# The first four levels of a triangular inverse: 32x32 block products in four row and column groups, in place of 64x64 products in two halves

## The chip, the cores and the metric

The kernel runs on one core of one Trainium2 chip. The metric is the device time of one execution in microseconds (us). Before the change three runs gave 1793.23 us as the median, from 1792.85 to 1796.31. The profile comes from one more execution, which took 1795.88 us.

## The reference

The reference is a stack of transformer blocks over 256 tokens of width 1024, in float32: two layers of a first kind (feed-forward, a mixer, cross attention, feed-forward), then two of a second kind. The change lies in the mixer of the first kind, in its recurrent branch with 8 heads of 64. Cut to what matters:

```python
def step(state, inp):
    r_t, w_t, k_t, v_t, kk_t, a_t = inp
    sa = jnp.einsum('bhij,bhj->bhi', state, -kk_t)
    state = (state * w_t[:, :, None, :] + sa[..., None] * (kk_t * a_t)[:, :, None, :]
             + v_t[..., None] * k_t[:, :, None, :])
    return state, jnp.einsum('bhij,bhj->bhi', state, r_t)
_, ys = lax.scan(step, state0, xs)          # 256 steps, once in each of the two layers
```

The kernel does not walk 256 steps. It cuts the sequence into 4 chunks of 64 tokens. Within a chunk the steps depend on one another by a strictly triangular 64x64 matrix for each head, and the chunk is solved at once with the inverse of (identity minus that matrix).

## The kernel before

**The whole.** Four engines run programs written out by hand, each strictly in its written order, and semaphores tie them together. TensorE (PE) multiplies; ScalarE (ACT) and VectorE (DVE) split each 128x1024 weight unit into a high part (L337) and a low part (L378), so that three fast products (L398, L399, L400) make one exact one, and they move results out of PSUM. SyncE (SP) streams the units through a ring of 4 buffers.

**The inverse.** Two token tiles `t` (128 partitions each) hold two chunks `c` each, the chunk in partitions 0 to 63 or 64 to 127, and 8 heads beside each other: 32 matrices of 64x64 in all, in `T2[t]`, which holds the inverse so far twice, straight and turned. `dve_rw_inv0` starts it with the inverses of the diagonal 2x2 blocks. Level `lv` (1 to 5) then joins the inverses of diagonal blocks of size 2^lv to such of twice that size. Each of the levels does this, first for t = 0 and then for t = 1 at each step:

- `pe_rw_level`, first loop ("level x"): X = M times T for every head and chunk, into the PSUM bank `x8(t)` (L1261). It waits for the T of the level before.
- `act_rw_level`: ScalarE copies the bank to SBUF, 128x512 (L1280).
- `pe_rw_level`, second loop ("level"): T times X into the same bank (L1273). It waits for that copy.
- `dve_rw_level`: VectorE takes only the new off-diagonal blocks over into T by a mask (COPY_PREDICATED, L1288), and for levels 1 to 4 transposes T by 32x32 blocks (STREAM_TRANSPOSE, L1292).

The masks `low1` to `low4` lie wholly within 32x32 diagonal blocks; `up5`, for level 5, is the 32x32 block off the diagonal.

**Products in halves.** Each product is 64x64 with 64 moving columns, from partitions of one chunk into the same partitions of PSUM. So two of them, c = 0 and c = 1, stand in different row and column groups of the array. A float32 product is two matmul instructions and two weight loads in the trace.

**What stands between the levels.** On PE, after level 2 and after level 3, 8 transposes of a "by token" matrix each (L1181); after level 4 the bonus products (L1417) and half a gate (L1429, L1430); then level 5, and the chunks of the recurrence (L1307 to L1370) with weight units between them. On VectorE each of the levels 1 to 4 is followed or preceded by a 128x1024 product (L1168, L1171, L1158) or a split (L378), in the order `dve_mix` has them:

```python
self.dve_rw_level(l, 1)
self.dve_rw_end(l, 0)
self.dve_split(1)
self.dve_rw_level(l, 2)
self.dve_rw_end(l, 1)
self.dve_rw_level(l, 3)
self.dve_rw_bonus(l)
self.dve_split(1)
self.dve_rw_level(l, 4)
self.dve_rw_level(l, 5)
```

On ScalarE a weight split (L337) stands before the copies of level 2 and of level 4.

Of the kernel before, what the change touches and what calls it, by code (L numbers as in the profile page):

```python
# [13 lines left out]
P = 128  # L14
# [8 lines left out]
HD = 64  # L23
# [108 lines left out]
class Program:  # L132
# [1118 lines left out]

    def pe_rw_level(self, l, lv):
        pe, m = self.nc.tensor, self.rw_pe
        for t in range(NT):
            pe.wait_ge(*self.rw_dve("T", l, t, lv - 1))
            if lv == 1:
                pe.wait_ge(*self.rw_dve("masked", l, 1, 2 * t))
            for h in range(8):
                for c in range(2):
                    co = slice(c * HD, (c + 1) * HD)  # L1260
                    ins = pe.matmul(self.x8(t)[co, h, :], self.MK[co, t, 2 * (h % 4) + h // 4, 0, :], self.T2[t][co, 1, h, :],  # L1261
                                    start=True, stop=True, skip_group_check=True)
            m.mark(ins, "level x", l, t, lv)
        for t in range(NT):
            T, X = self.T2[t], self.XG[t]
            pe.wait_ge(*self.rw_act("X", l, t, lv))
            if lv > 1:
                pe.wait_ge(*self.rw_dve("turned", l, t, lv - 1))
            for h in range(8):
                for c in range(2):  # L1270
                    co = slice(c * HD, (c + 1) * HD)
                    pair = (T[co, 0, h, :], X[co, h, :]) if lv < 5 else (X[co, h, :], T[co, 0, h, :])
                    ins = pe.matmul(self.x8(t)[co, h, :], *pair, start=True, stop=True, skip_group_check=True)  # L1273
            m.mark(ins, "level", l, t, lv)

    def act_rw_level(self, l, lv):
# [2316 lines left out]
```

## Time and profile before

| | |
|---|---|
| median of three runs | 1793.23 us |
| profiled execution | 1795.88 us, of it span 1794.6 |
| PE busy | 1771.5 us (99% of the span) |
| VectorE busy | 1153.2 us (64%) |
| ScalarE busy | 945.4 us (53%) |
| levels 1 to 4 of the inverse, layer 0 | 311.0 to 329.4 us |
| level 5, layer 0 | 333.3 to 338.8 us |
| levels 1 to 4, layer 1 | 934.4 to 952.8 us |
| level 5, layer 1 | 956.7 to 960.6 us |

### The profile page before, as it was taken

To read this page: it belongs to the slowest core of one execution; us is meant where nothing else is said; L and a number is where in the kernel's file an instruction comes from. 1 tells how busy PE (TensorE), PEld (TensorE's weight loads), DVE (VectorE), ACT (ScalarE), POOL (GpSimd) and SP (SyncE) were. 2 spreads that over 40 slices of the span, in tenths; PEclk is the share of its full clock that TensorE was granted. 3 is DMA by queue.
4 is the path that set the end of the run, shared out by engine and by line. 5 is a ranking of instruction groups with operands and counts; after the bars stand their busy time and mean duration, and the time that the engine had idled before them with its cause. 6 is when DMAs were issued, how large, how long until landed. Compare 5 with 4: busy or idle time off the path is not lost.

```text
span 1794.6 us, 26440 instructions
## 1 busy us (share of the span) xinstructions
PE 1771.5 (99%) x10810; PEld 1481.1 (83%) x10810; DVE 1153.2 (64%) x1577; ACT 945.4 (53%) x1433; POOL 130.1 (7%) x90
## 2 busy tenths in 40 slices
PE   9999999999999999999999999999999999999999
PEld 6888888878888888888888878888888888888887
DVE  5555688576555565556786755555697557697556
ACT  6454675345544454447653455444656554656553
POOL 0000010141000001000002310000002000002000
PEclk9999999999999999999999999999999999999999
DMA  8755542123555557545421336555554555554553
GB/s 288 279 187 188 176 143 93 61 94 119 189 186 187 188 185 250 187 170 188 141 84 61 127 110 228 188 188 171 169 176 157 172 188 192 179 176 152 174 187 133
DMA packets 84344, 301.14 MB, mean 168 GB/s; under 512 B 9728, under 2 KB 10880, under 8 KB 83712
## 3 DMA queue, kind: packets, MB, share of 16 engines
q1 hardware_dynamic: 80192, 289.44, 47.2%
q10 hardware_dynamic: 3712, 8.56, 1.4%
q8 instruction: 86, 1.41, 0.3%
q0 software_dynamic: 320, 1.45, 0.2%
q14 instruction: 34, 0.28, 0.0%
HBM read 298.36 MB, written 1.05 MB: 167 GB/s over the span
## 4 chain that ended last, share of the span: by engine, by line
PE 89%; DVE 6%; ACT 3%; issue 1%; DMA 1%; SPq 0%; DVEq 0%; ACTq 0%
PE ps L398 25%; PE ps L400 25%; PE ps L399 25%; DVE wlo L378 2%; PE ps L621 1%; PE ps L1273 1%; PE ps L1261 1%; DMA raw<-stream 1%; DVE a_lo L474 1%; ACT whi L337 1%; PE ps L2668 1%; PE ps L807 1%; PE ps L458 1%; PE ps L421 1%; PE ps L419 1%
## 5 line engine op out<-in xcount | busy, mean ns | idle before, releaser
L378 DVE TENSOR_TENSOR wlo<-raw,whi 128x1024 fp32r<-128x1024 f32 (+1 forms) x545 | 669.6, 1237 | 359.7 <-ACT whi L337 358.1
L337 ACT ACTIVATE whi<-raw 128x1024 fp32r<-128x1024 f32 (+1 forms) x545 | 570.9, 1053 | 455.7 <-PE ps L400 427.1
L398 PE MATMUL ps<-whi,a_hi 128*128 128x512 f32 x1712 | 678.5, 396 | 6.4 <-DVE a_lo L2003 2.0
L400 PE MATMUL ps<-whi,a_lo 128*128 128x512 f32 x1712 | 665.9, 389 | 0.0
L399 PE MATMUL ps<-wlo,a_hi 128*128 128x512 f32 x1712 | 665.0, 388 | 0.0
L398 PEld LDWEIGHTS ps<-whi,a_hi 128*128 128x128 f32 x1712 | 322.2, 188 | 75.8 <-issue 5.2
L400 PEld LDWEIGHTS ps<-whi,a_lo 128*128 128x128 f32 x1712 | 321.8, 188 | 67.5
L399 PEld LDWEIGHTS ps<-wlo,a_hi 128*128 128x128 f32 x1712 | 322.5, 188 | 61.4
L398 PE MATMUL ps<-whi,h_hi 128*128 128x512 f32 x336 | 131.7, 392 | 0.0
L400 PE MATMUL ps<-whi,h_lo 128*128 128x512 f32 x336 | 131.0, 390 | 0.0
L399 PE MATMUL ps<-wlo,h_hi 128*128 128x512 f32 x336 | 130.9, 389 | 0.0
L398 PEld LDWEIGHTS ps<-whi,h_hi 128*128 128x128 f32 x336 | 63.1, 188 | 13.6 <-issue 0.7
L419 PE MATMUL ps<-a_hi,whi 128*128 128x256 f32 x256 | 74.0, 289 | 0.0
L400 PEld LDWEIGHTS ps<-whi,h_lo 128*128 128x128 f32 x336 | 63.1, 188 | 13.2
L399 PEld LDWEIGHTS ps<-wlo,h_hi 128*128 128x128 f32 x336 | 63.1, 188 | 12.9
L420 PE MATMUL ps<-a_lo,whi 128*128 128x256 f32 x256 | 72.4, 283 | 0.0
L421 PE MATMUL ps<-a_hi,wlo 128*128 128x256 f32 x256 | 72.4, 283 | 0.0
L643 ACT ACTIVATE arena<-ps,small 128x256 f32<-128x256 f32 x88 | 36.9, 470 | 65.6 <-PE ps L400 65.5
L551 POOL TENSOR_TENSOR small<-small,minus_half 128x2 f32<-128x2 f32 x9 | 6.3, 700 | 858.0 <-DVE small L544 641.2
L689 DVE SCALAR_TENSOR_TENSOR arena<-ps,small,arena 128x256 f32<-128x256 f32 x88 | 38.5, 479 | 38.3 <-ACT arena L643 38.3
L650 ACT ACTIVATE h_hi<-ps 128x256 fp32r<-128x256 f32 x72 | 23.7, 382 | 57.3 <-PE ps L621 57.3
L788 POOL TENSOR_TENSOR small<-small,minus_half 128x16 f32<-128x16 f32 (+1 forms) x14 | 39.2, 2803 | 165.7 <-DVE small L2610 80.5
(332 smaller groups left out, 1688.4 us busy)
## 6 DMA issues: line engine op xcount, KB each, us to landing
raw<-stream SPq DMA_DIRECT2D x545, 512.0 KB, 3.3
arena<-rows ACTq DMA_DIRECT2D x2, 1026.0 KB, 14.8
arena<-mem_turned ACTq DMA_DIRECT2D x2, 1024.0 KB, 9.0
arena<-lora ACTq DMA_DIRECT2D x2, 768.0 KB, 6.5
arena<-x_turned SPq DMA_DIRECT2D x4, 256.0 KB, 5.9
x_res<-x SPq DMA_DIRECT2D x2, 512.0 KB, 9.1
arena<-mem ACTq DMA_DIRECT2D x1, 1024.0 KB, 14.2
arena<-rows ACTq DMA_DIRECT2D x2, 512.0 KB, 4.8
```

Of the source, the lines that this page charges most:

```text
L337: self.split_hi.mark(act.activation(self.weights(self.whi, u), self.weights(self.raw, u), ACT.Copy), u)
L378: self.split_lo.mark(dve.tensor_tensor(self.weights(self.wlo, u), self.weights(self.raw, u), self.weights(self.whi, u).bitcast(F32), ALU.s ...
L398: pe.matmul(out, a_h, hi, start=start, stop=False, skip_group_check=True)
L399: pe.matmul(out, a_h, lo, start=False, stop=False, skip_group_check=True)
L400: last = pe.matmul(out, a_l, hi, start=False, stop=True, skip_group_check=True)
L419: pe.matmul(out, hi, self.AHI[:, kt, :], start=first and kt == 0, stop=False, skip_group_check=True)
L420: pe.matmul(out, hi, self.ALO[:, kt, :], start=False, stop=False, skip_group_check=True)
L421: last = pe.matmul(out, lo, self.AHI[:, kt, :], start=False, stop=True, skip_group_check=True)
L643: self.silu.mark(act.activation(self.SG[:, t, :], self.bank((2 if j == 1 else 4) + t, 256), ACT.Silu, scale=self.rs(0, t)), key, j, t)
L650: self.ht_hi.mark(act.activation(self.h_place(j)[0][:, kk, :], self.bank(self.h_bank(j, kk), S), ACT.Copy), key, j, kk)
L689: self.h_ready.mark(dve.scalar_tensor_tensor(self.h_buffer(j)[:, t, :], self.bank((2 if j == 1 else 4) + t)[:, 256:512], self.rs(0, t), se ...
L788: m.mark(pool.tensor_tensor(x, x, self.minus_half[:, 0:x.shape[1]], ALU.pow), key)
```

## The change

For the levels 1 to 4 `size` becomes 32, and the list `blocks` has four pairs: rows 0 to 31 with columns 0 to 31, rows 32 to 63 with columns 32 to 63, rows 64 to 95 with columns 0 to 31, rows 96 to 127 with columns 32 to 63. Those are the four diagonal 32x32 blocks of the two chunks. The blocks off the diagonal are no longer computed; the bank keeps there what it held, ScalarE copies it along, and nothing reads it before level 5 has written the whole. In level 5 `size` is 64, and the list has the same two products as before. ScalarE, VectorE, GpSimd and SP are not touched; waits and signals stay where they were.

```diff
+        size = HD // 2 if lv < 5 else HD
+        blocks = [(slice(r, r + size), slice(r % HD, r % HD + size)) for r in range(0, P, size)]
         for t in range(NT):
...
             for h in range(8):
-                for c in range(2):
-                    co = slice(c * HD, (c + 1) * HD)
-                    ins = pe.matmul(self.x8(t)[co, h, :], self.MK[co, t, 2 * (h % 4) + h // 4, 0, :], self.T2[t][co, 1, h, :],
-                                    start=True, stop=True, skip_group_check=True)
+                for rows, cols in blocks:
+                    ins = pe.matmul(self.x8(t)[rows, h, cols], self.MK[rows, t, 2 * (h % 4) + h // 4, 0, cols],
+                                    self.T2[t][rows, 1, h, cols], start=True, stop=True, skip_group_check=True)
...
             for h in range(8):
-                for c in range(2):
-                    co = slice(c * HD, (c + 1) * HD)
-                    pair = (T[co, 0, h, :], X[co, h, :]) if lv < 5 else (X[co, h, :], T[co, 0, h, :])
-                    ins = pe.matmul(self.x8(t)[co, h, :], *pair, start=True, stop=True, skip_group_check=True)
+                for rows, cols in blocks:
+                    pair = (T[rows, 0, h, cols], X[rows, h, cols]) if lv < 5 else (X[rows, h, cols], T[rows, 0, h, cols])
+                    ins = pe.matmul(self.x8(t)[rows, h, cols], *pair, start=True, stop=True, skip_group_check=True)
```

The next rows are PE's order in the first layer, from the last weight unit ahead of the inverse to level 2 and the first transposes; - is before, + is after, and a count is one of products in the source, of which the trace has two instructions each:

```order
 L400 MATMUL ps<-whi,a_lo 128x512
-L1261 MATMUL ps<-arena 64x64 x32
-L1273 MATMUL ps<-arena 64x64 x32
-L1261 MATMUL ps<-arena 64x64 x32
-L1273 MATMUL ps<-arena 64x64 x32
+L1262 MATMUL ps<-arena 32x32 x64
+L1273 MATMUL ps<-arena 32x32 x64
+L1262 MATMUL ps<-arena 32x32 x64
+L1273 MATMUL ps<-arena 32x32 x64
 L1181 MATMUL ps<-const_tables,arena 128x128 x8
```

Nothing moves past anything else. Each group of 32 products (two tiles t of 16) becomes one of 64, each with half the rows, half the weight columns and half the moving columns.

## Rows read from the trace of the kernel before

**Rows 1.** The page: busy time of each engine, and the chain that ended last.

```profile
PE 1771.5 (99%) x10810; PEld 1481.1 (83%) x10810; DVE 1153.2 (64%) x1577; ACT 945.4 (53%) x1433; POOL 130.1 (7%) x90
PE 89%; DVE 6%; ACT 3%; issue 1%; DMA 1%; SPq 0%; DVEq 0%; ACTq 0%
```

**Rows 2.** Chain of waits, 311 to 338 us: start, duration, what.

```profile
311.04 2.01 PE ps L1261 x64
313.05 0.96 PE ps L1273 x32
...
317.33 1.87 PE ps L1273 x64
319.20 1.02 PE ps L1181 x8
...
327.39 2.08 PE ps L1273 x64
329.47 1.88 PE ps L1417 x16
...
333.37 3.40 PE ps L1261 x64
```

**Rows 3.** Timeline of VectorE, 314 to 338 us: start, duration, instruction, idle before it.

```profile
314.03 0.73 DVE L1288 COPY_PREDICATED arena<-const_tables,ps 128x512 f32<-128x512 int32 x1 [2.72 <-PE ps L1273]
...
317.90 1.21 DVE L378 TENSOR_TENSOR wlo<-raw,whi 128x1024 fp32r<-128x1024 f32 x1
319.03 0.73 DVE L1288 COPY_PREDICATED arena<-const_tables,ps 128x512 f32<-128x512 int32 x1
...
321.80 1.18 DVE L1171 TENSOR_TENSOR arena<-arena,small 128x1024 f32<-128x1024 f32 x1
323.31 0.73 DVE L1288 COPY_PREDICATED arena<-const_tables,ps 128x512 f32<-128x512 int32 x1 [0.33 <-PE ps L1273]
...
328.59 0.73 DVE L1288 COPY_PREDICATED arena<-const_tables,ps 128x512 f32<-128x512 int32 x1 [0.19 <-PE ps L1273]
...
337.91 0.73 DVE L1288 COPY_PREDICATED arena<-const_tables,ps 128x512 f32<-128x512 int32 x1 [6.48 <-PE ps L1273]
```

**Rows 4.** Timeline of ScalarE, 312 to 328 us.

```profile
312.17 0.60 ACT L1280 ACTIVATE arena<-ps 128x512 f32<-128x512 f32 x1 [4.42 <-PE ps L1261]
...
324.82 1.09 ACT L1188 ACTIVATE arena<-ps 128x512 f32<-128x512 f32 x2 [1.85 <-PE ps L1181]
325.79 1.06 ACT L337 ACTIVATE whi<-raw 128x1024 fp32r<-128x1024 f32 x1
326.74 1.14 ACT L1280 ACTIVATE arena<-ps 128x512 f32<-128x512 f32 x2
```

**Rows 5.** Windows of TensorE: stretch, length, busy (x in flight or started), clock.

```profile
299.95:299.98 0.03, 0.03 (x8) 1.00 0.00 0
299.98:300.06 0.09, 0.09 (x8) 1.00 0.00 0
300.06:300.08 0.03, 0.03 (x12) 1.00 0.00 0
```

**Rows 6.** Timeline of the tensor engine: L1209, L870's weight loads.

```profile
299.79 1.98 PE L1209 MATMUL ps<-arena 64*64 64x128 f32 x64
...
306.23 1.87 PEld L870 LDWEIGHTS ps<-arena 128*128 128x128 f32 x16
```

**Rows 7.** Windows, all engines: PE, PEld, DVE, ACT, POOL, then PEclk.

```profile
330.20:333.60 3.40, 3.40 (x25) 1.88 (x26) 1.19 (x2) 0.38 (x2) 0.00 (x0) 1.00 0.20 76
333.60:337.00 3.40, 3.40 (x72) 3.40 (x69) 0.00 (x0) 1.19 (x3) 0.00 (x0) 0.50 0.00 0
951.40:954.80 3.40, 3.40 (x68) 3.33 (x64) 3.14 (x5) 0.02 (x1) 0.00 (x0) 1.00 0.47 152
954.80:958.20 3.40, 3.40 (x55) 1.88 (x56) 0.01 (x1) 1.07 (x3) 0.00 (x0) 1.00 0.02 7
```

**Rows 8.** Chain of waits in layer 1, 956 us on.

```profile
956.76 2.01 PE ps L1261 x64
```

## The prediction, made before the changed kernel ran

> **What bounds the kernel now.** I read the busy shares and the chain of waits on the page first [rows 1]: PE is busy 99% of the span and carries 89% of the chain, so a saving on PE is a saving in time, except where PE waits for the others. Next I read the chain through the changed stage in layer 0 [rows 2]. It runs through PE in nearly every step: 64 matmul instructions of level 1's X take 2.01 us, 32 of the second loop 0.96, then VectorE's copy is waited for once. Then the engines beside it: VectorE [rows 3] waits 2.72 us for PE in level 1, not at all in level 2 (its copy at 319.03 begins the moment the split of 317.90 is done), and 0.33 and 0.19 us in levels 3 and 4. So levels 1 to 4 are two chains of nearly the same length, PE's and VectorE's. This is what decides the worth of the change: whatever PE gains, VectorE allows only a part of it. ScalarE has gaps, but one place is tight: before level 4 it does the by-token copies (324.82), a split (325.79, 1.06 us) and only then the X copies (326.74) [rows 4].
>
> **The price of one product.** In the levels PE starts 64 matmul instructions in 1.87 us (the row at 317.33) [rows 2]: 29 ns each. As two halves of the array work side by side, one half takes a new one every 58 ns. The weight load is the likely limit of it: 16 loads of 128 columns take 1.87 us [rows 6], 117 ns each or 0.91 ns a column, and 64 columns at that rate are 58 ns. Nothing in the trace is 32x32, so I bound the new product from both sides.
>
> - Low end: four groups side by side, each with 32 columns of load and 32 of stream: 32 x 0.91 = 29 ns a round, perhaps 33 with a fixed part. For this to hold four instructions must be able to start in 29 ns. They can at least in a burst: L1209 uses four 64x64 positions; in a window of 0.03 us 4 new ones are added to the 8 in flight, and none in the 0.09 us before it, so four start at once every 0.11 us [rows 5]. A batch (one t of one loop) has 8 heads x 4 blocks x 2 = 64 instructions, so 16 rounds: 0.47 to 0.53 us, against 0.93 now (32 instructions x 29 ns).
> - Middle: a round stays at 58 ns, because something fixed limits a product this small. 16 x 58 ns = 0.93 us, no change.
> - High end: no more is started in the long run than the trace ever shows. The four of L1209 every 0.11 us [rows 5] are 27 ns each, and over its whole run of 64 it is 1.98 us [rows 6], 31 ns with the last one's own duration; the levels have 29. A batch is then 64 x 27 to 29 ns = 1.75 to 1.87 us, twice that of now.
>
> I take 0.53 us. Four do start within 0.03 us, and both streams of 27 and 29 ns are explained by the columns that they stream and load, so they set no limit on starts. It is the weakest step.
>
> The Trainium skill speaks against the change in two places, and these sentences can be left out. "TensorEngine Tiling (Array Packing)", section Performance Considerations, says each matmul has an overhead of about 60 cycles, one free column costing as much as 60; an estimate by that is the middle case, 0.93 us. "TensorE: Matmul & The Clock Gate", section "Wait — 56ns, not 53.3ns?", gives a floor of about 25 ns from start to start however few columns; were it to hold across tiles too, the estimate is 64 x 25 = 1.6 us a batch. The four starts within 0.03 us in L1209 contradict the second for a burst; no row tests it in a long stream of short ones.
>
> **What the change is worth, step by step (layer 0).** PE's own work falls by 16 batches x 0.40 = 6.4 us a layer. What of it lies on the path I work out by moving the measured instructions, with the measured durations of the other engines:
>
> - Level 1. X of t=0 ends 0.35 earlier, so ScalarE's copy starts at 311.8 instead of 312.17 [rows 4]; with the copy's 0.60 and a second batch 0.35 shorter, VectorE's first copy comes at 313.3 instead of 314.03 [rows 3]: 0.7 gained.
> - Level 2. VectorE was back to back and stays so: its copy moves from 319.03 to 318.3. Gained still 0.7. PE now waits for it.
> - Level 3. VectorE's 0.33 us of waiting goes, since PE's second loop ends about 321.9 and VectorE is free at 322.3: copy at 322.3 instead of 323.31. Gained 1.0.
> - Level 4. The wait of 0.19 goes too; VectorE is free at 327.5, against 328.59: 1.1. PE is ahead of it: the by-token transposes end at 323.6, ScalarE copies and splits until 325.5, copies X to 326.6, and PE's last batch starts at 326.75 and ends its starts at 327.3. Before, that was 329.3 (327.39 + 1.87) [rows 2].
> - After level 4 PE does not wait for VectorE: the bonus products need nothing of this level. So the path from here is PE's, and it is 2.0 us early. Level 5 needs VectorE's T of 329.7, and PE comes to it at 331.3 instead of 333.37. The gain carried on is 2.0 us, and PE leads through the chunks after it.
>
> Level 5, the copies, the transposes, all waits and all DMAs stay as they are; 1024 more matmuls and 1024 more loads over both layers add to fetching of instructions, which I price at nothing because the stage has the same length; if the cover is gone, it is in the high case. The switch of array shape stands where it stood, between 128-row products and the levels, and I take its cost as unchanged. Two layers: 4.0 us.
>
> **The clock takes some back.** In layer 0 the granted clock is 1.00 while PE does bonus and gate at 330 to 333.6, and 0.50 (the lower level, 1.2 GHz) behind that, at 333.6 to 337.0 [rows 7]. There 64 instructions of level 5 take 3.40 us [rows 2] instead of 2.01 in layer 1 [rows 8]; the price is 1.4 us. In layer 1 the same work at 951 to 958 kept 1.00 [rows 7]. With the change the levels ahead of the bonus have PE idle or working on a quarter of the rows at a time, so there is less work ahead of the same lull. I expect layer 0 to have its slow stretch as before and layer 1 to get one too: 1.4 us back. Sum: 4.0 - 1.4 = 2.6 us faster. The profiled execution would go from 1795.88 to 1793.3. It was 2.65 us above the median of the three runs; against that median the forecast is 1793.23 - 2.6 = 1790.6.
>
> **Rivals.**
>
> - B, the round stays at 58 ns: the batches are as long as now, the order is the same, nothing moves. Time 1793.2, with 1 us either way for the clock. For it: a small product's duration is mostly fixed. Against it: both rates above go by columns.
> - C, starts limit the stream (slower). Place: the 16 batches of the levels. Price at the high end: PE needs 4 x 1.8 = 7.2 us a level, and with two sets of transposes (1.02 each) 30.8 us where the stage takes 18.4 now, so 12.4 a layer and 25 in all: 1818. It decides from a batch of 1.0 us on, since PE's own work in the stage now is 16 x 0.93 + 2 x 1.02 = 16.9 of 18.4: a batch of 1.2 us makes it 21.2, 2.8 more a layer and 6 in all: 1799. For it: no row shows a long stream faster than 27 ns a start. Against it: the burst.
> - D, the clock falls within levels 2 to 4 too. Then a batch is 1.06 us, about today's, the two sets of transposes, the bonus and the gate take twice as long for a stretch: +1 us for each set, +1.9 for the bonus. With two such stretches the whole gain is gone: 1792 to 1796. For it: less work in each microsecond. Against it: by-token transposes with all rows keep standing between.
> - E, VectorE becomes the bound wholly and the 0.9 us that PE gains beyond VectorE's 1.1 is lost at level 5: then 1.1 a layer, 2.2 in all, before the clock: 1792. Against it: VectorE waits 6.48 us for level 5's products (the last row) [rows 3].
>
> **How the numbers follow.** The forecast (with four groups side by side, clock costs of 0 to 2.5 us): 0.50. B 0.14; C 0.20, spread from 1796 to 1820; D 0.10; E 0.06. A measurement of this kernel tells about 0.2%, 3.6 us, from no change. Faster than 1789.6 asks for the forecast's own mechanism with no clock cost: somewhat over half of its 0.50, 0.28. Slower than 1796.8 is nearly all of C and a little of D: 0.21. The rest, 0.51, is within. The range: low 1787, where the forecast gains 4.0 and layer 0's slow stretch goes as well (1793.2 - 4.0 - 1.4 = 1787.8) with a little beyond. High 1799, which takes in B, D, E and the mild part of C, and leaves out the rest of C, about 0.15.
>
> **What would show it.** Right: 64 instructions of 32x32 start in about 0.5 us; PE idles in the levels, for VectorE's copy in L1288 and for ScalarE's in L1280; VectorE's copy of level 4 stands 1.1 us closer to the start of level 1, level 5 2.0 us closer; level 5's products or the gate are at 0.50 in both layers. Wrong: 64 starts in 0.9 us or more (B, C), or the clock at 0.50 between levels 1 and 4 (D). The forecast fails first if the starts fail: that is one number, the spacing in a batch.

## The result, and the profile after

The changed kernel takes 1823.93 us (median of 3 runs, 1823.87 to 1825.05) against 1793.23 before: ratio 1.0162, 95% interval 1.0147 to 1.0177, slower by some 30 us. Its profiled execution took 1823.93 us with a span of 1822.6, 28.0 above the span before. The forecast was 1790.6, the range 1787 to 1799.

The page after, the busy line and the chain [rows 1]:

```profile
PE 1779.4 (98%) x11834; PEld 1483.6 (81%) x11834; DVE 1153.8 (63%) x1577; ACT 946.2 (52%) x1433; POOL 131.2 (7%) x90
PE 89%; DVE 6%; ACT 2%; issue 2%; DMA 0%; SPq 0%; DVEq 0%; ACTq 0%
```

PE has 1024 more matmuls and as many more weight loads; "issue" in the chain has gone from 1% to 2%. That is a rounded hint at what the chain of the stage shows in full. The chain of waits of the changed kernel, layer 0, with start, duration and what (columns as in [rows 2]):

```profile
310.95 0.70 PE ps L1262 x50
...
312.32 0.78 PE ps L1273 x50
...
313.12 0.75 DVE arena L1288
...
313.91 0.37 PE ps L1262 x18
314.28 2.73 issue
317.02 1.70 PE ps L1262 x107
318.72 0.36 PE ps L1273 x18
319.08 1.55 issue
320.63 1.71 PE ps L1273 x110
...
325.77 1.89 issue
...
332.64 1.96 issue
...
336.65 2.20 issue
338.85 0.26 PE ps L1273 x2
339.11 3.50 PE ps L1417 x16
```

Two things are to be seen. Level 1 goes as forecast: PE's two loops take 0.6 us a batch, and VectorE's first copy comes at 313.12 instead of 314.03. Then, 18 matmuls into level 2, PE stops for 2.73 us, and it stops four more times before the bonus products, each time in the middle of a batch and with no semaphore behind it: 10.3 us in layer 0. "Issue" means that the engine waited for nothing that the profile shows. The bonus starts 28.16 us behind the start of level 1, instead of 18.43 [rows 2]. Layer 1 has five such stops as well, 9.7 us, and the bonus at +27.95.

What PE waits for stands beside the stops. Windows of the changed kernel in layer 1, where the first stop is (columns as in [rows 7]):

```profile
950.80:951.50 0.70, 0.00 (x0) 0.00 (x0) 0.67 (x2) 0.25 (x1) 0.00 (x0) 1.00 0.45 181
951.50:952.60 1.10, 0.00 (x0) 0.00 (x0) 0.33 (x1) 0.00 (x0) 0.00 (x0) 0.71 0.05 15
952.60:953.90 1.30, 0.00 (x0) 0.00 (x0) 0.00 (x0) 0.00 (x0) 0.00 (x0) 0.50 0.00 0
954.00:955.00 1.00, 0.99 (x74) 0.99 (x76) 0.37 (x1) 0.00 (x0) 0.00 (x0) 0.50 0.00 0
```

The DMA view for the second of these windows, and then for 950 to 978 us (queue: packets, MB, share):

```profile
q8 instruction: 1, 0.02, 5.4%
...
GB/s 345 222 29 0 0 0 0 23 0 0 0 0 23 140 357 252 0 23 0 0 0 0 23 0 0 0 0 0 23 0 0 0 0 70 263 357 82 23 0 0
...
q8 instruction: 8, 0.13, 1.9%
```

At 950.8 the first level's second loop breaks off; a packet of instructions is moved in the window 951.5 to 952.6; PE starts again at 954.0. In the longer view (0.7 us a column) the six lone 23s are such packets, and two more lie within weight transfers: 8 in 28 us, 3.5 us apart on average, never two together. The page's line of this queue, before and after (packets, MB, share):

```profile
q8 instruction: 86, 1.41, 0.3%
...
q8 instruction: 94, 1.54, 0.3%
```

A packet is 16 KB, and 1024 matmuls with 1024 loads more made 8 more of them, so one holds 256 PE instructions. Every run below agrees: 1024 instructions less gave 82 packets, 256, 512 and 768 more gave 87, 88 and 89, and 6144 more gave 110. Batches of 0.55 us consume 128 in that time, 256 in 1.1 us; they arrive every 3.5 us.

The granted clock falls as well, in the stops and after them. Windows after, layer 0:

```profile
310.90:317.00 6.10, 3.04 (x275) 2.71 (x275) 4.13 (x7) 2.14 (x3) 0.00 (x0) 1.00 0.26 89
317.10:323.90 6.80, 5.25 (x246) 4.98 (x245) 3.39 (x5) 1.68 (x3) 0.00 (x0) 0.50 0.26 82
...
334.20:351.20 17.00, 14.41 (x237) 11.10 (x238) 2.88 (x4) 2.57 (x5) 0.00 (x0) 0.50 0.10 33
```

Half of the first window PE was idle; at 0.50 (1.2 GHz) it then ran most of level 2 and its transposes, and later the second loops of levels 3 and 4, the bonus, the gate and most of level 5. The mean granted clock over the span is 0.984, against 0.998 before: some 58 us at half speed instead of 7 (an estimate from the two means and spans).

**Where the 28.0 us went**, both layers: up to the bonus +9.7 and +9.5, in which there are 20.0 us of stops; bonus and gate at half clock, 7.42 us instead of 3.90, +3.5 each; level 5 +0.6 and +1.2. That makes 28.0; the stretches between the layers and after them are as long as before.

### The profile page after: what moved, and what is told of

The parts are those of the page before. It is cut to its first block, busy times and chain, and to the rows that moved or that the text cites. A ratio compares the mean times of both kernels' runs of the same rounds, so it can differ in the third digit from the quotient of the medians.

```text
span 1822.6 us, 28488 instructions
## 1 busy us (share of the span) xinstructions
PE 1779.4 (98%) x11834; PEld 1483.6 (81%) x11834; DVE 1153.8 (63%) x1577; ACT 946.2 (52%) x1433; POOL 131.2 (7%) x90
## 4 chain that ended last, share of the span: by engine, by line
PE 89%; DVE 6%; ACT 2%; issue 2%; DMA 0%; SPq 0%; DVEq 0%; ACTq 0%
PE ps L398 25%; PE ps L400 25%; PE ps L399 25%; DVE wlo L378 2%; PE ps L621 1%; PE ps L1262 1%; PE ps L1273 1%; DVE a_lo L474 1%; PE ps L2668 1%; PE ps L807 1%; PE ps L458 1%; ACT whi L337 1%; PE ps L421 1%; PE ps L419 1%; PE ps L420 1%
## 5 line engine op out<-in xcount | busy, mean ns | idle before, releaser
L398 PEld LDWEIGHTS ps<-whi,a_hi 128*128 128x128 f32 x1712 | 321.9, 188 | 75.4 <-issue 3.7
```

The lines of the kernel that those rows point to most:

```text
L398: pe.matmul(out, a_h, hi, start=start, stop=False, skip_group_check=True)
```

## The experiments

Three theories: F, PE runs out of instructions, which come 256 at a time every 3.5 us at best; M, the 32x32 tiles stall PE themselves; C (K in one text), the granted clock, which falls when PE has little to do. Each ratio is to the kernel before on the same chip and beside the run; there it took 1795.6 to 1796.0 us in the median, not 1793.23, and single runs of it 1792.6 to 1799.6. So small differences are read from the ratios, and ranges in us that start from 1793 lie some 3 us low. `+` with a number is a time behind the start of level 1.

**Two of the four blocks** (`e1_two_of_four`): 32x32 tiles, but as many instructions as before. Half of the blocks is left out.

```diff
-        blocks = [... for r in range(0, P, size)]
+        blocks = [... for r in range(0, P, HD)]
```

> Levels 1 to 4 compute only one 32x32 block of each chunk (rows 0 to 31 and 64 to 95), so half of the blocks is left out; the products are 32x32, but PE has as many instructions as before the change. Theory F (PE runs out of instructions: they arrive 256 at a time every 3.5 us): no idle on 'issue' within the levels, batches of 0.5 us, level 5 about 2 us earlier than before the change, total 1787 to 1794. Theory M (the 32x32 products themselves, or the change of array shape, stall PE): gaps of 1.5 to 3 us in each level stay, total above 1805.

Measured 1805.97 us, ratio 1.0054 (1.0037 to 1.0071). PE's timeline:

```profile
311.49 1.20 PE L1262 MATMUL ps<-arena 32*32 32x32 f32 x64
312.88 1.20 PE L1273 MATMUL ps<-arena 32*32 32x32 f32 x64 [0.19 <-ACT arena L1280]
314.41 0.69 PE L1262 MATMUL ps<-arena 32*32 32x32 f32 x32 [0.32 <-DVE arena L1288]
315.76 0.75 PE L1262 MATMUL ps<-arena 32*32 32x32 f32 x32 [0.66 <-DVE arena L1288]
316.31 1.95 PE L1273 MATMUL ps<-arena 32*32 32x32 f32 x64
318.19 1.97 PE L1181 MATMUL ps<-const_tables,arena 128*128 128x128 f32 x8
...
329.63 3.57 PE L1417 MATMUL ps<-const_tables,arena 128*128 128x2 f32 x16
```

The stops on "issue" are gone; what idle is left is the wait for VectorE and ScalarE that the forecast had. So M falls, although the time alone is what M had (above 1805). But it is 10 us above before, not at 1787 to 1794, so F alone isn't enough either. From 316.31 on everything is at half clock (8 transposes 1.97 us, 1.02 before). Windows of the same run:

```profile
311.50:316.30 4.80, 3.62 (x193) 3.29 (x194) 2.95 (x5) 2.64 (x4) 0.00 (x0) 1.00 0.29 113
316.30:329.60 13.30, 13.03 (x346) 12.07 (x340) 11.89 (x15) 6.10 (x10) 0.52 (x1) 0.50 0.17 55
```

The clock stayed down for 23.9 us in each layer, and the bonus came at +18.14 instead of the forecast's +16.4. Bonus and gate took 7.4 us instead of 3.9. So the clock can fall without any stop; why it fell the run doesn't tell.

**64x64 products, each twice** (`e2_64_twice`): the changed kernel's number of instructions, in the old tiles.

```diff
+        blocks = blocks * 2 if lv < 5 else blocks      # size = HD in all levels
```

> Levels 1 to 4 with the 64x64 products of before, each issued twice: as many PE instructions as the changed kernel, but PE is busy with each for 29 ns. Theory F: 128 instructions a batch take 1.7 us to arrive and 1.87 us to run, so no long idle; the stage grows by 16 x 0.93 - 1.5 = 13.4 us a layer, total 1793 + 27 = 1820, and the granted clock stays at 1.0 in the levels. Theory K (most of the loss of the changed kernel is the clock, not the instructions) expects the same 1820 here, but then the changed kernel without its slow clock would be near 1793; the share is read from the idle on 'issue' of this run and of the changed one.

Measured 1826.14 us, ratio 1.0167 (1.0152 to 1.0182).

```profile
310.74 3.95 PE L1263 MATMUL ps<-arena 64*64 64x64 f32 x128
314.52 3.90 PE L1274 MATMUL ps<-arena 64*64 64x64 f32 x128
318.25 3.90 PE L1263 MATMUL ps<-arena 64*64 64x64 f32 x128
```

256 instructions are run in 3.73 us, just over the 3.5 in which they arrive: no stop but one of 0.27 us, and the clock at 1.0 to the gate. The stage grew by 14.4 us (bonus at +32.9), 1 more than expected. It is as slow as the changed kernel, though in another way: at full clock a batch takes PE 0.6 us there and 1.9 here, and the rest of the time there is stops and slow clock. It doesn't say how the changed kernel's loss splits between F and C.

**Each 32x32 product twice** (`e7_four_blocks_twice`): the slope.

```diff
+        blocks = blocks * 2 if lv < 5 else blocks      # size 32 in levels 1 to 4
```

> The changed kernel with each 32x32 product of levels 1 to 4 issued twice: 2048 more PE instructions a layer. Theory F (PE gets 256 instructions every 3.5 us at best, whatever they do): 8 more packets a layer, 28 us each layer, total 1824 + 56 = 1880, with instruction packets 3.4 to 3.6 us apart through the stage. If PE were limited by what it runs: 16 batches more a layer of 0.53 us at full clock or 1.06 at half, 17 to 34 us, total 1841 to 1858.

Measured 1887.74 us, ratio 1.0505 (1.048 to 1.053): 64 above the changed kernel, where F had 56 and the running time at most 34. A piece of its chain of waits in layer 0, where `issue` comes once in every packet:

```profile
343.44 1.29 PE ps L1263 x79
344.73 0.11 PE ps L1274 x7
344.85 1.89 issue
346.74 1.93 PE ps L1274 x125
348.67 1.67 issue
350.34 1.83 PE ps L1274 x120
```

From stop to stop there are 3.6 to 3.8 us and about 125 matmuls here, that is 250 instructions with their loads; the packets through the stage were 3.3 to 4.1 us apart, where I had 3.4 to 3.6. 4096 instructions of the stage took 58.6 us, 3.66 us per 256. This is the strongest sign for F: twice the instructions, twice the stage (28.2 to 58.6), at the same products.

**32x32 in fewer places** (`e3_level1`, `e4_level1_and_4b`, `e12_level4b`). The edits choose `size` by level and loop:

```diff
-        size = HD // 2 if lv < 5 else HD
+        size = HD // 2 if lv == 1 else HD            # e3: both loops of level 1; e4: also the second loop of level 4
+        size = HD // 2 if lv == 4 else HD            # e12: only the second loop of level 4
```

> 32x32 blocks in level 1 only, the other levels in 64x64: 256 more PE instructions a layer than before the change. Theory F: PE begins the stage with instructions in stock (the changed kernel ran level 1 without a gap in layer 0 and all but 25 instructions of it in layer 1), so level 1 gains 0.8 us on VectorE's copy and at most a gap of 1 to 2 us follows in level 2: total 1790 to 1796. Theory M: a gap of about 3 us a layer after level 1, 1798 or more.

> 32x32 blocks in level 1 and in the second loop of level 4, which is followed by stretches with few instructions (bonus and gate): 384 more PE instructions a layer than before. Theory F: level 4's second loop gains 0.8 us on PE's path if the instructions are there, and loses up to 1.5 us if they are not: total 1788 to 1797. Theory M: gaps after both, 1802 or more.

> 32x32 blocks only in the second loop of level 4, which the bonus and the gate follow with few instructions: 128 more PE instructions a layer than before. If they are there in time, PE's path gains 2 x 0.4 us a layer and nothing else moves: ratio 0.9985 to 1.000. Theory F: instruction packets were 3.4 us apart ahead of that place before the change too, so a gap of up to 1.5 us a layer can follow: ratio up to 1.002. Theory C: the lull of bonus and gate gets a little longer, so a slow stretch of 1.4 us may join in layer 1.

Measured: e3 1800.82 us, ratio 1.0031 (1.0018 to 1.0044); e4 1802.13, 1.0032 (1.0020 to 1.0044); e12 1797.76, 1.0012 (1.0001 to 1.0024). All are slower than before, e12 only just clear of it. e12 is within what F had (a ratio up to 1.002). e3 and e4 lie beyond F's ranges, by 2 to 3 us if the ratios are put on 1793.23 and by 5 as measured, and the measured times are those that I had given M (1798 or more, 1802 or more). The times don't decide here, the place of the stop does. In e3, layer 0, the stop after level 1 falls among products that are 64x64 again, which M can't explain:

```profile
314.09 0.79 PE L1262 MATMUL ps<-arena 64*64 64x64 f32 x18 [0.24 <-DVE arena L1288]
316.65 2.62 PE L1262 MATMUL ps<-arena 64*64 64x64 f32 x46 [1.77 <-issue]
```

So the stock at the start of the stage is about one level's worth; in layer 1 the stop is 3.2 us and comes within level 1. A gain of 0.8 us on VectorE's first copy is paid with 1.8 and 3.2, and the clock falls behind the stop. e4 stops for 1.5 us in layer 0, and for 1.8 and 0.7 in layer 1. In e12 there is no stop, and the gain came: bonus at +17.70 and +17.84 instead of +18.43. The lull of bonus and gate then lost the clock in both layers for 6.8 us, level 5 with it (the profiled execution took 1800.96 us, 3 above the median of its eleven runs):

```profile
328.80:333.50 4.70, 4.70 (x24) 2.45 (x20) 2.38 (x4) 0.18 (x1) 0.00 (x0) 0.81 0.36 115
333.60:338.50 4.90, 4.90 (x94) 4.90 (x96) 0.00 (x0) 1.79 (x3) 0.00 (x0) 0.50 0.02 3
```

No version with 32x32 blocks beat the kernel before.

**Added work** (`e5_after_filled`, `e6_before_filled`, `e8_two_of_four_filled`).

```diff
+    def pe_rw_fill(self, n=2):                       # called after levels 1, 2 and 3
+        for _ in range(n):
+            self.nc.tensor.matmul(self.bank(2), self.C[:, 0:P], self.C[:, 0:512], start=True, stop=True, ...)
```

> The changed kernel, and after each of the levels 1, 2 and 3 two products of 128x128 by 512 columns on constant tables into a bank that is free there (8 PE instructions and about 1.9 us of work each time, result unused). Theory F (256 instructions every 3.5 us): the added work falls into the time in which PE has no instructions, so the stage does not grow, and where it keeps the granted clock at 1.0 it shrinks: level 5 at +26 to +29 us behind the start of the stage, total 1812 to 1824. If the gaps of the changed kernel came from anything that must end before the next product may start, the added 5.7 us a layer come on top: 1835.

> The kernel before with the same added products, as the control. PE has only some 1.5 us of idle a layer in the stage there, so nearly all of 5.7 us a layer shows: level 5 at +26 to +27 instead of +22.3, total 1796 + 9 = 1805. Were this as cheap as in the changed kernel, the filled run of that would say nothing on instructions.

> The run with two of the four blocks (half of the blocks left out, as many PE instructions as before), with the added products of the filled runs. Theory C (the granted clock falls when PE has little to do, and that alone cost the two-of-four run its 10 us): the added work holds the clock at 1.0 and hides where PE waits for VectorE, so the stage is shorter than in the two-of-four run although PE does more: level 5 at +22 to +24 instead of +25.6, total 1792 to 1799. Without C the added work can only add: 1803 to 1812.

Measured: e6 1804.08 us, ratio 1.0044 (1.0029 to 1.0059), as expected. e5 1832.08, 1.0201 (1.0184 to 1.0218), 8 us above the changed kernel (7 by the ratios), where I expected none: near the 1835 that I had given the rival in which something must end before the next product starts. The added work cost here nearly what it cost in e6, so by the terms of e6's text the time of e5 is no evidence for F. e8 1804.93, 1.0055 (1.0038 to 1.0071), no better than the run without added work, and in the range that I had for "without C".

The miss of e5 corrects F in one point. In layer 0 the bonus came 1.6 us later than in the changed kernel, in layer 1 5.6 us; the stops fell from 10.3 to 6.0 us in layer 0, but only from 9.7 to 8.7 in layer 1. Its chain of waits in layer 1:

```profile
951.60 3.13 issue
...
955.47 3.71 PE ps L1278 x4
...
961.78 2.75 issue
...
965.33 3.71 PE ps L1278 x4
```

A stop of about the old length (2.75 us) follows the added products (L1278) all the same, and these took 3.71 us at half clock, not the 1.9 of full clock. The instruction packets were 3.3 to 3.9 us apart where there was a stop and 4.8 to 6.4 us where the added work lay. So packets did not come ahead as time allowed: the next seems to be asked for only when PE has got through a part of the last, since it begins to move about 1.1 us after PE starts again (954.0 to 955.1 in the changed kernel), and PE gets on 2.4 us after that. That the request hangs on progress is read from these spacings; no run moved it alone.

In e8, layer 0, the clock held to the end of the bonus (1.0 up to 331 us, against 316 without the added work), and the bonus came at +18.4, only 0.3 later in spite of 5.7 us more of work. In layer 1 the clock fell within the last batches of level 4 already, and the bonus took twice as long:

```profile
329.59 1.88 PE ps L1422 x16
...
953.40 3.50 PE ps L1422 x16
```

Level 5 came at +24.2 in layer 0, against +25.6 without the added work and +22 to +24 in my text, and at +26.1 in layer 1, against +25.7. So the added work held the clock in the levels, as C says, and saved nothing in sum, because the clock fell behind them.

**Half of the heads in 64x64** (`e10_half_the_heads`): a light PE without small tiles.

```diff
-            for h in range(8):
+            for h in (range(4 * (1 - lv % 2), 8 - 4 * (lv % 2)) if lv < 5 else range(8)):
```

> Levels 1 to 4 in 64x64 products as before the change, but for only 4 of the 8 heads (in turn the first and the last four; the others' blocks are left out): half the PE instructions, batches of 0.47 us, no 32x32 tile. Theory C: the clock falls here too, in some stretches, since PE is idle half of the stage; total 1793 to 1803. If instead the clock depends on the small tiles alone, it stays at 1.0 and the path is the forecast's: level 5 at +20.3 instead of +22.3, total 1790 to 1793.

Measured 1791.23 us, ratio 0.9981 (0.9968 to 0.9993): 3 to 4 us faster than before, with half of the work of the levels left out. Windows of its profiled execution, which took 1798.09 us, the slowest of its ten:

```profile
311.00:326.60 15.60, 11.80 (x274) 10.08 (x273) 13.63 (x18) 8.51 (x14) 0.53 (x1) 1.00 0.22 69
326.60:332.80 6.20, 6.20 (x25) 3.19 (x22) 3.10 (x5) 0.18 (x1) 0.00 (x0) 0.61 0.26 87
```

This is the forecast's timing come true with batches of half the length and no lack of instructions: the bonus at +15.6 instead of +18.43, 2.8 us a layer where I had worked out 2.0. Level 5 came at +21.8 and +20.9, where I had +20.3. In the levels the clock held with PE busy 11.80 of 15.60 us, the same share as in the first window of the two-of-four run (3.62 of 4.80), after which it fell. The products differ: 64x64 at two positions here, 32x32 there. That this is the cause is not shown, since the two runs differ in the times of their products as well. Behind the levels the clock fell in the lull here too, so neither of the two cases in the text above came out whole.

## Why the prediction was wrong, point by point

- **The price of one product** was right. I took 0.53 us a batch from 0.47 to 0.53 and from 1.75 to 1.87; measured, a stretch with instructions at hand and the clock at 1.0 has 64 matmuls in 0.54 to 0.61 us, four starts every 32 ns. What I called the weakest step, the starts, held: they go on at 8 ns, and 64 starts in 0.9 us, my sign of B and C, came only at half clock. The floor of 25 ns from start to start that the Trainium skill gives ("TensorE: Matmul & The Clock Gate", section "Wait — 56ns, not 53.3ns?") does not hold across products side by side: they start 8 ns apart. The overhead of 60 cycles a matmul in the Trainium skill ("TensorEngine Tiling (Array Packing)", section Performance Considerations) is 25 ns at 2.4 GHz, an estimate from the page's figure. Each place of the array starts a matmul every 32 ns here, so this run does not contradict it, and my estimate by it, the middle case of 58 ns a round, did not follow from it.
- **The step that failed** was the sentence in which I priced the fetching of 2048 more instructions "at nothing because the stage has the same length". The stage had 1024 of them in 18.4 us, a packet every 4.6 us on average, and packets took no less than 3.4; with 2048 it needs 8 packets, 28 us at 3.5. It took 28.16 and 27.95. A packet could come only 25% sooner, and I doubled the number of packets; nor did the stage have the same length in my own sum, which made it shorter. The trace before showed it: the DMA view of 320 to 328 us has two instruction packets, in levels 3 and 4, and narrow windows put them at 321.9 and 325.3, 3.4 us apart.

```profile
q8 instruction: 2, 0.03, 1.5%
```

- **Rival C** had the place, the sign and nearly the size (a batch at 27 to 29 ns a start, 1818), but a wrong mechanism: I set it against the bursts of L1209 and gave it 0.20. 3.5 us for 128 matmuls is 27 ns, the pace that I had from L1209. The limit was of the supply and not of the starts. That the two figures are the same is not explained by any run: L1209's stream was 64 matmuls, half a packet.
- **The moves beside it** were right as far as they could be tested: level 1's copy moved 0.8 us forward (forecast 0.7), and the run with half the heads gave 2.8 us a layer to the bonus (forecast 2.0).
- **The clock** was mis-sized. I gave 1.4 us for one more slow stretch in layer 1. The changed kernel spent some 50 us more at 1.2 GHz; bonus and gate alone cost 7.0 us more in the two layers. Rival D, for which I had 0.10, came true in its place, the levels 2 to 4, and was dearer than its 1792 to 1796: in the two-of-four run, without any stop, a forecast gain of 2.6 us became a loss of 10.
- What stays open is how the 28 us split between stops and clock in the levels themselves: a stop lowers the clock, and a low clock makes the work between the stops longer, which shortens the stop. The stops are 20.0 us, bonus, gate and level 5 at the low clock 8.8; up to the bonus the stage grew by 19.2, less than the stops in it, so within the levels the two hide each other.

## What to carry to other kernels

Cutting a product into smaller ones that run side by side multiplies TensorE's instructions, and they have a supply of their own: here 256 every 3.5 us, 14 ns each, a matmul with its load 27 ns. Before splitting, divide the instructions of the stage (matmuls and loads) by 256 and set the packets of the instruction queue against its length. And where TensorE's work gets lighter in front of a lull, count the lull at half clock: in the runs with 32x32 products and no lack of instructions (e1, e12) that cost more than the products saved.

## What the runs showed of the hardware

- 32x32 products (float32, 32 moving columns) at four places of the array: four matmul instructions start every 32 ns, and a product is two of them; 64 start in 0.54 to 0.61 us.
- PE's instructions come in packets of 16 KB, 256 instructions. In a stretch that consumes them faster, packets are 3.3 to 4.1 us apart (3.5 on average in the changed kernel, 3.66 in the run with twice the products); PE stops for up to 3.3 us in each, and in the changed kernel starts again 2.3 to 2.8 us after the packet has begun to move. The profile calls the stop "issue".
- The granted clock fell to 0.50 after a stretch of 32x32 products with PE busy 3.62 of 4.80 us (75%), and held under 64x64 products at 11.80 of 15.60 (76%).
